# One block of 96 tokens in place of two kinds of block, in a mixture-of-experts stage on TensorE

## The reference, cut to what matters

```python
def moe_ffn(h, w_router, b_router, w_gate_up, b_gate_up, w_down, b_down):
    logits = (h @ w_router).astype(jnp.float32) + b_router
    topv, idx = lax.top_k(logits, TOP_K)                       # 4 of 32
    gates = jax.nn.softmax(topv, axis=-1)
    ...
    def expert_block(args):
        xblk, e = args
        gu = xblk @ w_gate_up[e] + b_gate_up[e]                # 1024 -> 2 * 1024
        gate = jnp.minimum(gu[:, :D_FF], SWIGLU_LIMIT)
        up = jnp.clip(gu[:, D_FF:], -SWIGLU_LIMIT, SWIGLU_LIMIT)
        act = (up + 1.0) * (gate * jax.nn.sigmoid(SWIGLU_ALPHA * gate))
        return act @ w_down[e] + b_down[e]                     # 1024 -> 1024
```

## Time and profile before

| | |
|---|---|
| median of the runs | 3157.84 us |
| the profiled execution's span | 3155.9 us |
| TensorE (PE) busy | 2956.2 us, 94% of the span |
| weight loads (PEld) busy | 2056.7 us, 65% |
| VectorE (DVE) busy | 1215.3 us, 39% |
| ScalarE (ACT) busy | 751.5 us, 24% |
| GpSimd (POOL) busy | 116.9 us, 4% |
| the expert stage on TensorE | from 719.48 us to 1805.0 us |

### The profile page before, as it was taken

The page is one execution under the profiler, slowest core; times in us unless marked ns, Lnnn a source line. Parts: engine busy times, 40 slices in busy tenths (PEclk is TensorE's granted clock), DMA queues, the critical chain, the costliest instruction groups (busy, mean ns, idle before and its releaser), DMA issues.

```text
span 3155.9 us, 43167 instructions
## 1 busy us (share of the span) xinstructions
PE 2956.2 (94%) x15320; PEld 2056.7 (65%) x15321; DVE 1215.3 (39%) x2572; ACT 751.5 (24%) x1483; POOL 116.9 (4%) x132
## 2 busy tenths in 40 slices
PE   8989899998999999899899879898999999999999
PEld 7874667655585556386357668586776596776774
DVE  6770773242212221211212156535333355444432
ACT  3221751111212121211211023514111225232111
POOL 0000100000000000000000000011000000110000
PEclk9999999988999999999999989899999999999999
DMA  4222012257999999999999452021321220112221
GB/s 171 81 67 79 3 41 80 74 204 298 395 364 365 419 413 390 416 379 382 408 415 391 149 201 95 1 87 49 108 84 54 100 95 27 61 61 87 81 80 67
DMA packets 137804, 577.60 MB, mean 183 GB/s; under 512 B 15981, under 2 KB 21485, under 8 KB 87504
## 3 DMA queue, kind: packets, MB, share of 16 engines
q1 hardware_dynamic: 128176, 558.87, 46.6%
q0 software_dynamic: 9504, 17.07, 1.4%
HBM read 572.47 MB, written 20.97 MB: 188 GB/s over the span
## 4 chain that ended last, share of the span: by engine, by line
PE 85%; DVE 5%; DMA 5%; ACT 2%; issue 2%; DVEq 1%; SPq 0%; POOLq 0%; ACTq 0%
PE banks L395 31%; PE banks L1521 13%; PE banks L1497 9%; PE banks L332 8%; PE banks L1027 7%; PE banks L1471 6%; DMA arena<-in_w_experts 5%; PE banks L800 3%; PE banks L823 2%; PE banks L811 2%; PE banks L271 1%; DVE arena L873 1%; DVE arena L885 1%; PE banks L1451 1%; PE banks L1926 1%
## 5 line engine op out<-in xcount | busy, mean ns | idle before, releaser
L395 PE MATMUL banks<-arena 128*128 128x256 f32 (+2 forms) x4704 | 1015.3, 377 | 21.6 <-ACT arena L432 7.4
L395 PEld LDWEIGHTS banks<-arena 128*128 128x128 f32 x4704 | 883.8, 192 | 142.0 <-issue 21.5
L1521 PEld LDWEIGHTS banks<-arena 128*128 128x128 f32 x3584 | 403.8, 193 | 14.5 <-issue 14.5
L1521 PE MATMUL banks<-arena 128*128 128x128 f32 x3584 | 405.5, 277 | 4.7 <-issue 4.7
L1497 PE MATMUL banks<-arena 128*64 128x512 f32 (+1 forms) x1024 | 322.6, 593 | 0.0
L1471 PE MATMUL banks<-arena 128*64 128x512 f32 x1152 | 268.3, 616 | 24.9 <-DMA arena<-in_w_experts 22.3
L1599 DVE TENSOR_TENSOR arena<-banks,arena 128x512 f32<-128x512 f32 x64 | 44.3, 692 | 614.1 <-PE banks L1521 351.9
L432 ACT ACTIVATE arena<-banks 128x512 f32<-128x512 f32 (+2 forms) x168 | 98.7, 588 | 690.9 <-PE banks L395 690.9
L448 DVE TENSOR_TENSOR arena<-banks,arena 128x512 f32<-128x512 f32 (+2 forms) x126 | 85.7, 680 | 436.2 <-PE banks L395 434.7
L332 PE MATMUL banks<-arena 128*128 128x512 f32 x576 | 250.0, 593 | 0.0
L1497 PEld LDWEIGHTS banks<-arena 128*64 128x64 f32 (+1 forms) x1024 | 123.5, 159 | 176.1 <-issue 176.0
(11 more groups left out here) (210 smaller groups left out, 2041.0 us busy)
## 6 DMA issues: line engine op xcount, KB each, us to landing
arena<-in_w_experts SPq DMA_DIRECT2D x384, 1024.0 KB, 19.3
arena<-in_w_in SPq DMA_DIRECT2D x84, 1024.0 KB, 5.0
arena<-in_w_out SPq DMA_DIRECT2D x12, 1024.0 KB, 5.0
arena<-in_w_branch SPq DMA_DIRECT2D x24, 512.0 KB, 4.7
arena<-expert_rows SPq DMA_DIRECT2D x4, 2048.0 KB, 14.4
arena<-in_w_in SPq DMA_DIRECT2D x4, 832.0 KB, 4.6
arena<-in_gate_b SPq DMA_DIRECT2D x2, 1536.0 KB, 6.5
arena<-in_x SPq DMA_DIRECT2D x4, 512.0 KB, 5.3
```

The lines of the kernel that those rows point to most:

```text
L395: last = PE.matmul(PS[:, bank, t * width:(t + 1) * width], one[:, t * P:(t + 1) * P], other, start=(first and t == 0 and kk == 0), stop=(t ...
L1521: last = PE.matmul(PS[:, q, f * P:(f + 1) * P], gate_up(q, k)[:, f * P:(f + 1) * P], xT[:, k], start=(f == 0 and k == 0), stop=(f == 3 and ...
```

## The change

A block is now 96 tokens (`BS`), and every block is worked in one way, with no branch. Of its 96 token columns the first 64 go the short block's way, in two column halves. The last 32 are added behind each part: with 32 tokens as the stationary operand, the array's columns are used as four groups of 32, and each group streams its own 256 columns of weights (`more_products`, and the new lines in `down`). ScalarE copies one more 128 x 256 result per half into a new buffer (`GV_`), TensorE turns it with four more transposes per half, and ScalarE's copy of the block's result grows from two instructions (short) or one (full) to six. An expert can now have up to six blocks in the lists instead of four, so the lists are 192 columns wide instead of 128; the block number is worked out by another scaling of the position.

```diff
+BS = 96
+LPE = -(-S // BS)
...
-MAXBLK = S * TOPK // P + NE
+MAXBLK = S * TOPK // BS + NE
...
-        LISTS = TT * NE
+        LISTS = LPE * NE
...
-                for b in range(TT):
+                V.scalar_tensor_tensor(row_f, blk_f, -float(BS * PART), addrf, ALU.mult, ALU.add)
+                for b in range(LPE):
                     V.scalar_tensor_tensor(v(R + 1856 + 16 * b, 16), blk_f, float(b), v(CO["slot1"], 16), ALU.is_equal, ALU.mult)
                 V.drain()
-                for b in range(TT):
+                for b in range(LPE):
                     V.tensor_tensor(slots[:, :, b], oh, v(R + 1856 + 16 * b, 16).unsqueeze(2).to_broadcast([P, 16, NE]), ALU.mult)
...
+                    def more_products(h, ks):
+
+                        for k in ks:
+                            for g in range(4):
+                                last = PE.matmul(PS[QB * g:QB * (g + 1), 3 - h, 0:256], xT[:, k, HB:BS],
+                                                 gate_up(2 * h + g // 2, k)[:, 256 * (g % 2):256 * (g % 2) + 256],
+                                                 start=(k == 0), stop=(k == 7), tile_position=(0, QB * g))
+                        return last
...
+                        if more:
+                            for f in range(2):
+                                for s in range(2):
+                                    half = slice(HB * s, HB * (s + 1))
+                                    to = PS[:, 2 * h + s].rearrange("p (a f t) -> p f a t", a=2, f=2)
+                                    last = PE.transpose(to[:, f, :, HB:BS], v(GV_ + 256 * h + f * P, P, HB, HB * s),
+                                                        ident[half, half])
                         last.then_inc(SEM["gu_rdy"], 1)
...
                             if f % 2 == 1:
+                                if more:
+                                    for ff in (f - 1, f):
+                                        for g in range(4):
+                                            last = PE.matmul(PS[QB * g:QB * (g + 1), 7 - g // 2, 0:256], aT[:, ff, HB:BS],
+                                                             down_rows(ff)[:, 256 * g:256 * g + 256],
+                                                             start=(ff == 0), stop=(ff == 7), tile_position=(0, QB * g))
                                 last.then_inc(SEM["ch_free"], 1)
...
-                    with pe.If(few > 0):
+                    def rows_of_block(more):
                         for h in range(2):
                             for kh in range(2):
+                                ks = range(4 * kh, 4 * kh + 4)
                                 arrived(part(2 * h, 4 * kh))
                                 arrived(part(2 * h + 1, 4 * kh))
                                 if h and kh:
-                                    turn_products(0)
-                                products(h, range(4 * kh, 4 * kh + 4)).then_inc(SEM["ch_free"], 2)
-                        turn_products(1)
+                                    turn_products(0, more)
+                                last = products(h, ks)
+                                if more:
+                                    last = more_products(h, ks)
+                                last.then_inc(SEM["ch_free"], 2)
+                        turn_products(1, more)
                         gather_T(j + 2)
-                        down(lambda n: (PS[HB * n:HB * (n + 1), 6 + n], HB))
-                    with pe.Else():
...
+                        down(more)
+
+                    rows_of_block(True)
...
+                    def rows_of_block(more):
                         for h in range(2):
                             act.wait_ge(SEM["ch_free"], up(12 * j + 16 + 4 * h))
                             apart(act, 12 * j + 16 + 4 * h)
-                            AC.activation(v(GU_ + 512 * h, 512), PS[:, 4 + h], ACT.Copy).then_inc(SEM["gu_out"], 1)
+                            last = AC.activation(v(GU_ + 512 * h, 512), PS[:, 4 + h], ACT.Copy)
+                            if more:
+                                last = AC.activation(v(GV_ + 256 * h, 256), PS[:, 3 - h, 0:256], ACT.Copy)
+                            last.then_inc(SEM["gu_out"], 1)
                             gate(h)
                         copy_T(j + 2)
                         rows_ready()
                         AC.activation(v(Y_, 512, HB), PS[0:HB, 6], ACT.Copy)
-                        AC.activation(v(Y_ + 512, 512, HB), PS[HB:P, 7], ACT.Copy).then_inc(SEM["y_rdy"], 1)
...
+                        last = AC.activation(v(Y_ + 512, 512, HB), PS[HB:P, 7], ACT.Copy)
+                        if more:
+                            for g in range(4):
+                                last = AC.activation(v(Y_ + 256 * g, 256, QB, HB), PS[QB * g:QB * (g + 1), 7 - g // 2, 0:256], ACT.Copy)
+                        last.then_inc(SEM["y_rdy"], 1)
```

More of the change, by code:

```diff
@@ L28 @@
 LIMIT, ALPHA = 7.0, 1.702
-MAXBLK = S * TOPK // P + NE
+BS = 96
+LPE = -(-S // BS)
+WAYS = 1 << 14
+PART = -(-WAYS // BS)
+MAXBLK = S * TOPK // BS + NE
 MLA_SCALE = 96 ** -0.5
@@ L1258, in pe_ @@
                 pe.wait_ge(SEM["column_rdy"], up(1))
-                for q, col in enumerate((TAB + 352, TAB + 356, TAB + 357)):
+                for q, col in enumerate((FOUND, FOUND + 4, FOUND + 5)):
                     last = PE.matmul(PS[0:1, 1, 64 * q:64 * q + 64], v(col, 1), ident[:, 0:64], start=True, stop=True)
@@ L1332, in dve_ @@
                 cnt, nb, cum = v(TAB, NE), v(TAB + 32, NE), v(TAB + 64, NE)
[L1333 to L1338, removed]
+                t1 = v2(TAB + 96, NE, LPE)
+                step = v(TAB + 96 + NE * LPE, NE)
+                past = v2(TAB + 128 + NE * LPE, 3, NE)
+                found = v(FOUND, 3)
+                bef, stf, left = (v(FOUND + q, 1) for q in range(3))
+                of, few, row = v(FOUND + 4, 1), v(FOUND + 5, 1), v(FOUND + 6, 1)
                 V.tensor_copy(cnt, PS[:, 1, 128:160])
@@ L1420, in expert_stage @@
             J = MAXBLK + 2
-            HB = P // 2
+            HB, QB = P // 2, P // 4
             def nblocks(eng):
@@ L1482, in turn_products, with down @@
                                                     v(GU_ + 512 * h + f * P, P, HB, HB * s), ident[half, half])
+                        if more:
[5 more added lines that the diff above has]
+                                                        ident[half, half])
                         last.then_inc(SEM["gu_rdy"], 1)
-                    def down(place):
+                    def down(more):
                         pe.wait_ge(SEM["y_rdy"], up(j))
@@ L1495, in down @@
                             for n in range(2):
-                                to, tokens = place(n)
-                                last = PE.matmul(to, aT[:, f, 0:tokens], down_rows(f)[:, n * 512:(n + 1) * 512],
-                                                 start=(f == 0), stop=(f == 7))
+                                last = PE.matmul(PS[HB * n:HB * (n + 1), 6 + n], aT[:, f, 0:HB],
+                                                 down_rows(f)[:, n * 512:(n + 1) * 512], start=(f == 0), stop=(f == 7))
                             if f % 2 == 1:
+                                if more:
[4 more added lines that the diff above has]
+                                                             start=(ff == 0), stop=(ff == 7), tile_position=(0, QB * g))
                                 last.then_inc(SEM["ch_free"], 1)
-                    with pe.If(few > 0):
+                    def rows_of_block(more):
                         for h in range(2):
                             for kh in range(2):
+                                ks = range(4 * kh, 4 * kh + 4)
                                 arrived(part(2 * h, 4 * kh))
@@ L1507, in pe_ @@
                                 if h and kh:
-                                    turn_products(0)
-                                products(h, range(4 * kh, 4 * kh + 4)).then_inc(SEM["ch_free"], 2)
-                        turn_products(1)
-                        gather_T(j + 2)
-                        down(lambda n: (PS[HB * n:HB * (n + 1), 6 + n], HB))
-                    with pe.Else():
[L1514 to L1532, removed]
+                                    turn_products(0, more)
[4 more added lines that the diff above has]
+                        turn_products(1, more)
+                        gather_T(j + 2)
+                        down(more)
+                    rows_of_block(True)
             def act_(act, c):
@@ L1565, in act_ @@
                         AC.activation(v(Y_, 512, HB), PS[0:HB, 6], ACT.Copy)
-                        AC.activation(v(Y_ + 512, 512, HB), PS[HB:P, 7], ACT.Copy).then_inc(SEM["y_rdy"], 1)
[L1567 to L1572, removed]
-                        AC.activation(y, PS[:, 6:8].rearrange("p a b -> p (a b)"), ACT.Copy).then_inc(SEM["y_rdy"], 1)
```

(3 more changed lines are left out.)

36 lines of the change are left out of this document (15 added, 21 removed).

## The result

The changed kernel takes 3249.61 us (two runs, 3248.32 to 3250.91), against 3157.84 before: 1.0296 of it, with a 95% interval of 1.028 to 1.0313. It is slower by 3.0%, and the forecast was 3256 us. The profiled execution lasts 3246.4 us, 90.5 more than the one of before.

What follows compares the result with a forecast made beforehand. It took the stage as TensorE-bound, plus 46.7 us of weight waits. Stage +93 us, router +4, tail +1.7: +98.7 on the profiled 3155.9, the median 1.9 above, gives 3256 us; its own range 3210 to 3322.

Steps and rivals of the forecast that it cites:

- The count of blocks and what bounds them: Expert stage before: 18 short blocks of 23.69 us, 14 full of 43.22, bound by TensorE, plus 46.7 us waiting for weights.
- The four-group passes: Gate, up and down products: 48 sets of four passes a block, each set 0.217 us, adding 10.4 us a block.
- the dearer case: Rival for the four-group products: four run at a time but a set costs 0.30 us; 3384 us, chance 0.09.
- Two at a time: Rival for the four-group products: only two groups run together, a set costs 0.43 us; 3589 us, chance 0.13.
- The changes of shape: TensorE's changes of column use, 8 at 0.12 us and 6 at 0.15, adding 1.9 us a block.
- not slower: Rival: changes between halves and quarters are free; 3195 us, or 3190 without the issue gap; chance 0.12.
- Turns and ScalarE's second copy: Four more TensorE turns per half, 0.25 us for both; TensorE's wait for the second copy in half 1, 0.38 us.
- The block: Every block of the expert stage takes 36.6 us: a short one 12.9 dearer, a full one 6.6 cheaper.
- The gap of 4.7 us at the loop's first turn: Issue time where the loop first met a full block; kept in the sum, with bounds 0 and 4.7 us.
- The router: Ahead of the stage: list operations +1.3 us, router passes over 192 columns +2.4, smaller operations +0.3; together +4 us.
- The tail: Behind the stage: the last block's copy goes from 1.02 to 2.7 us, +1.7 us.
- The transfers: An expert's weights need 30.3 us, less than a 36.6 us block, so the 46.7 us of waits go.

Runs made afterwards that it cites:

- e4_before_half_bytes: Kernel before, with only half of each 1 MB weight chunk brought in for every expert but the first: 3114.86 us, ratio 0.9862.
- e6_group_outer: Changed kernel with all four-group passes of one column group in a part issued before the next group's, same products: 3591.56 us, ratio 1.1386.
- e3_more_once: Changed kernel with the four-group products gathered, once behind each half of gate and up and once behind the down product: 3208.2 us, ratio 1.0155.
- e1_branch: Changed kernel with the branch back, so blocks of up to 64 tokens leave out the four-group part: 3114.01 us, ratio 0.987 to the kernel before.
- e7_before_96_columns: Kernel before, with 96 instead of 128 token columns streamed in the full block's gate and up products: 3157.05 us, ratio 1.0003.
- e8_branch_once: Changed kernel with the branch back for short blocks and the four-group products gathered behind each half and behind the down product: 3118.8 us, ratio 0.9887.
- e9_branch_quarters_first: Changed kernel with the branch back and, in the last part of down, four-group records ahead of the 64-column ones: 3110.28 us, ratio 0.9857.

## Why the prediction was right

The forecast was +98.7 us on the profiled execution; it came to +90.5. The mechanism was right and so was the size of the large terms; one small term failed, and one came near for another reason than the one given. By its own steps:

*The count of blocks and what bounds them.* 32 blocks, 18 of 23.7 and 14 of 43.2 us before, as counted from the groups. e4_before_half_bytes takes the waits for weights away by themselves: the stage falls by 42.8 us, and the blocks that had waited by 41.4, where 46.7 had been ascribed to the waits. Of the difference, 2.3 us lie in the second block of the kernel before, which takes 45.51 us at a granted clock of 0.95 and not 43.22; the prediction allowed for the clock in the first block only. The rest is 0.1 to 0.2 us in many blocks.

*The four-group passes, 10.4 us a block.* Right. The first starts of one part of the changed kernel lie at 0, 7, 13 and 20 ns, the next four 240 ns later and then every 216 ns, against the 217 taken from full-array passes. Four groups cost the time of one; the dearer case of 0.30 us a set is not there. Two at a time would have made a block about 47 us; e6_group_outer shows such a block, reached by nothing but the order of the products. So this forecast hung on an order that keeps a group's waiting passes at three or fewer, which the prediction did not know: it said only that TensorE looks past a waiting record, "how far is not shown". The in-order rule that was quoted there from the Trainium skill, page "TensorE: Matmul & The Clock Gate", section "Step-by-step: what each phase is for", is not what this kernel's traces show: matmuls of other column groups start ahead of waiting ones in front of them, up to three for each group (e6_group_outer).

*The changes of shape, 1.9 us a block.* Right, and what separates this forecast from the rival "not slower": by e3_more_once a change costs 0.145 us, so that 14 of them are 2.0 us. Changes between halves and quarters are not free, although all 128 rows stay in use. The decision point was 0.06.

*Turns and ScalarE's second copy, 0.25 and 0.38 us.* The added turns take 0.12 and 0.13 on the chain. The copy (L1569) stands there with its 0.39, but the wait from the last product to the turn grows from 0.85 to 1.13 only, because ScalarE starts it (820.33) before its first copy is done (819.84 + 0.60). So 0.28 us in place of 0.38.

*The block, 36.6 us.* Measured 36.6.

*The gap of 4.7 us at the loop's first turn, kept in the sum.* This term failed. The changed kernel has no such gap: its blocks follow one another at once. With the branch back, the chain of e1_branch shows it again, at the same place, the first block that takes the other side:

```profile
745.17 4.86 issue
750.03 5.78 PE banks L1473 x16
```

It belongs to the branch. Its length is no constant: 4.73, 5.45 and 3.11 us in three traces of the old branch (before, e7_before_96_columns, e4_before_half_bytes), 4.86, 4.96 and 5.70 in those of the new one. The list of DMA packets makes the fetch of the other side's code likely: a 16 KB transfer of instructions starts at 745.68 us in the kernel before and at 745.09 in e1_branch, as the gap opens, four more follow within 35 us, and then there is none until the stage is over. But the list doesn't say for which engine they are, the first takes 1.1 us and not 4.8, and no run isolates it.

*The router, +4 us.* Too high. L1259 (L1255 before) grew from 5.28 to 8.22, but from the products ahead of it to the start of the stage it is 26.39 us against 26.03. The two extra list operations of VectorE hid behind L1206's products, and the first gather took 4.64 instead of 6.47 us. The stage starts 2.8 us later; 2.4 of these had come about ahead of the router's products, in work that the change doesn't touch. Only 0.4 us came about from there on, so that 2.8 lies near the forecast's 4 is luck.

*The tail, +1.7 us.* From the last product to the first sum it takes 15.25 us instead of 13.45: +1.8.

The sum as measured: 2.8 ahead of the stage, 88.2 in it, 1.8 behind it, and 2.3 less in the rest of the program: 90.5. The 2.3 have no term and no known cause; the two executions of the changed kernel differ by 2.6. The forecast was 8.2 us too high by the gap (4.7), the router (1.2) and these.

*The transfers.* The prediction said that 36.6 us is more than the weights need, which holds. Its price, 30.3 us an expert, was too low; with gather and scatter it is 32.3. That didn't touch this forecast, but it is the main reason why the expectation for e1_branch was 29 us or more too fast.

What the change got wrong is visible in the sum by kind: it makes each of 14 full blocks 6.6 us cheaper (92 us) and takes away 41 us of waits and the 4.7 of the gap, but makes each of 18 short blocks 12.9 us dearer (232 us), and these are the ones that needed none of it. Leaving the addition out where there are 64 tokens or fewer (e1_branch) turns 3.0% slower into 1.3% faster.

## What to carry to other kernels

When a change replaces two paths by one in between, price each by the trace and multiply by its count before looking at what is simpler; here the cheap path was the common one. A stage can sit close to two bounds at once: a gain on the engine then stops where the transfers stand, and their price is all that goes through the queues, not the weights alone. When passes are spread over column groups, issue the groups in turn, and run as many products of one shape in a row as the buffers allow.

## What the runs showed of the hardware

- Four column groups of 32 run side by side in float32 at the time of one full-array pass: 216 ns for 256 columns.
- Each column group holds up to three waiting passes while passes of other groups start ahead of them; a fourth blocks what stands behind it. With 8 passes of one group in a row a part took 4.53 us instead of 1.86, with 4 in a row 1.02 instead of 1.00.
- A change of TensorE between products that use the columns in halves and in quarters costs 0.145 us in the mean (e3_more_once, nine changes fewer, 36.6 to 35.3 us a block).
- A full-array float32 pass over 96 columns takes as long as one over 128 (405.0 and 405.5 us for 3584 of them).
- A block that ends in 16 short records within 1.0 us leaves 0.81 to 0.99 us of issue ahead of the next one when a branch follows (e1_branch); ending in 64 such records over 3.59 us it leaves 0.43 to 0.61 (e8_branch_once), and ending in 8 records over 1.87 us none (e9_branch_quarters_first). That the sequencer lacks a lead behind short records is the reading that fits; it was not measured by itself.
- With a branch in the loop, the first block that takes the other side is preceded by 3.1 to 5.7 us of issue, once; without a branch there is no such gap.
